# Gating z where the projection's tiles leave PSUM, key rows and index scores in one block, prompt attention with turning three steps behind

## The chip, the cores and the metric

One core of one Trainium2 chip runs the kernel. The metric is device time in microseconds (us) from the start to the end of one execution, and the number compared is the median of several runs. Engine names: TensorE (PE in the rows, its weight loads PEld), VectorE (DVE), ScalarE (ACT), GpSimd (POOL), SyncE (SP, issues DMAs). A "q" behind a name (SPq, ACTq) marks what the engine's sequencer issues.

## The reference

One inference step of a two-layer decoder: a prompt of 512 tokens and 8 sample sequences of one token each (a past of 2048). Layer 0 has two attention mixers on one input projection; layer 1 is a gated convolution. For this change the following matters, in the reference's own lines (cut):

```
def att_project(h, w_in):
...
    proj = h @ w_in
...
    ga = jax.nn.sigmoid(ga).reshape(b, t, G_A, R_A, 3)
...
    wi = wi * (H_IDX ** -0.5)
...
def dsa_select(qi, wi, kidx, t, topk):
    dots = jnp.einsum('bqhd,bld->bqhl', qi, kidx, preferred_element_type=jnp.float32) * (D_IDX ** -0.5)
    score = jnp.einsum('bqh,bqhl->bql', wi.astype(jnp.float32), jax.nn.relu(dots))
...
def att_merge(ga, za, zb, o_cmp, o_slc, o_win, o_b, w_out):
    b, t = za.shape[:2]
    o_a = ga[..., 0:1] * o_cmp + ga[..., 1:2] * o_slc + ga[..., 2:3] * o_win
    o_a = o_a.reshape(b, t, -1) * jax.nn.silu(za)
    o_b = o_b.reshape(b, t, -1) * jax.nn.silu(zb)
    return jnp.concatenate([o_a, o_b], axis=-1) @ w_out
```

The projection's columns are split into qa, kc, vc, ks, vs, kw, vw, ga, za, qb, kb, vb, qi, wi, ki and zb; the new rows of the keys and values and of ki are outputs of their own. silu(z) = z / (1 + exp(-z)). za and zb are 8 heads of 128 columns each, so 16 of the projection's 66 tiles are z tiles.

## The kernel before, in words

Activations lie transposed: 128 rows of features by 520 columns (512 prompt tokens, 8 sample tokens; `TC = 520`). The work is a row of stages; each is one block with a program per engine, and ends with the clearing of its semaphores and a barrier of all engines (`stage`, L90).

**Projection** (`stage_project`, L474). 66 tiles of 128 output columns. For tile t ScalarE makes the high part of the weights (`hi`, L128), VectorE the low part (`lo`, L133), TensorE runs 96 matmuls (L146), ScalarE copies the left half of PSUM to `pj_out` (L567) and VectorE the right half (L609), GpSimd stores the tile to the DRAM tensor `proj` (L635). Weight parts have two buffers, so `hi` and `lo` of tile t+2 start when tile t is done and are needed when tile t+1 is done. After every second tile TensorE also does two slots of the next conditioning product (L199). `SEGS` cuts the 16 rounds of four tiles into loops.

**Rows** (`stage_rows`, L647). Nine groups of key or value tiles, then the tile of gates (`GW`), are loaded from `proj` (L667 to L671), turned by TensorE (L687, L688), copied by VectorE (L704 to L708) and stored to the outputs from ScalarE's queue (L718, L722). SyncE waits for each load to land before it issues the next.

**Sample queries** (`stage_sample_queries`, L726). The sigmoid of the gates, one load of all tiles' sample columns (`sT`, L736, 8320 runs of 32 bytes), ten small loads of gates through DRAM (L740 to L744) issued by SyncE, and 33 small VectorE instructions (L773 to L779).

**Index scores of the prompt** (`stage_index_prompt`, L798). For 16 heads: load q (L817), four matmuls (L831), Relu on ScalarE (L842), multiply-add on VectorE (L854); at the end GpSimd cuts the diagonal (L863). Then the stage of sample index scores begins (L912, `stage_index_sample`).

**Prompt attention** (`stage_attend_prompt`, L1699), once for mixer A (two branches) and once for B. Two groups of four heads; a head is 8 (A) or 4 (B) units of 128 query rows with 128 to 512 keys. A step t in program order: TensorE does the logits of unit t (L1790), turns the probabilities of unit t-DT (L1804) and multiplies those of unit t-DV by the values (L1818). VectorE adds bias and takes the maximum (L1877 in A; L1880 and L1883 in B), negates it (L1885), then normalizes unit t-1 (L1892, L1896 or L1898). ScalarE scales the queries of the next head (L1827), takes exp (L1846) and copies turned probabilities out of PSUM (L1860). In A a compressed branch comes with each head's first unit (L1786, L1815). z of a head: exp on ScalarE (L1830), plus one on GpSimd (L1995), the reciprocal on VectorE in four (A) or two (B) pieces, one a step (L1905), times z on GpSimd (L1997), and the product with the attention output at the head's end (L1948, L1950). `SL` is the number of heads whose loads have a buffer: 2 in A, 4 in B. Loads of a head wait for the head that used the buffer to finish (`fin`).

```
DP, DT, DV, ring = 1, 2, 3, 4
SL = 2 if A else 4
```

Of the kernel before, what the change touches and what calls it, by code (L numbers as in the profile page):

```python
# [473 lines left out]
def stage_project(k):  # L474
# [7 lines left out]
    SEGS = [(0, 1, 0, 0, 2 * D), (1, 4, 512, 0, 2 * D + 512), (4, 5, 2048, 1, 0), (5, 13, 2584, 1, 512), (13, 14, 2584 + 8 * 512, 1, 9 * 512), (14, 16, 7208, 1, 10 * 512)]  # L482
# [12 lines left out]
    with ExitStack() as ctx:  # L495
# [3 lines left out]
        heads = k.sb("pj_heads", [2 * NH, BREV], ctx=ctx)  # L499
        ada = Ada(k, ctx, 4, "1")  # L500
        with nc.Block() as block:
# [57 lines left out]
            def _(act):  # L559
# [8 lines left out]

                def body(j, seg):
                    for s in range(4):  # L570
                        step(4 * seg[0] + s, j, first=(seg[0] == 0))
                    ada.keep_rows(act, ada_entry(4 * seg[0] + 3), seg[0], j, 2)
                    if seg[0] == 5:
                        copies(j)
# [21 lines left out]
                step(64, 0)  # L596
                step(65, 0, last=True)
# [32 lines left out]
            def _(pool):  # L630

                def store(t, j4, tile):
                    pool.wait_ge(kept_a, j4 + (t + 3))
                    pool.wait_ge(kept_v, j4 + (t + 3))
                    pool.dma_start(tile, out[:, t % 4, :]).then_inc(stored[t % 4], 16)  # L635

                with pool.Fori(0, 16) as j:
# [7 lines left out]


def stage_rows(k):  # L647

    nc, ps = k.nc, k.psum
    tile_in, turned, rows_kept, rows_out, table_in = (k.sem(f"rw_{n}") for n in ("tile_in", "turned", "rows_kept", "rows_out", "table_in"))  # L650
    pairs = [(KC, "cmp_k"), (VC, "cmp_v"), (KS, "slc_k"), (VS, "slc_v"), (KW, "win_k"), (VW, "win_v"), (KB, "dsa_k"), (VB, "dsa_v"), (KI, "idx_k")]
    with ExitStack() as ctx:
# [3 lines left out]
        with nc.Block() as block:  # L656

            @block.sync
            def _(sp):
                sp.dma_start(k.pages[:, :], k.i["page_table"].rearrange("(o s) p -> o (s p)", o=1)).then_inc(table_in, 16)  # L660
                sp.dma_start(k.hot[:, :], k.i["hot"][:, T:O_ALL]).then_inc(table_in, 16)
                for n, (tile, name) in enumerate(pairs + [(GW, None)]):
                    if n >= 2:

                        sp.wait_ge(turned, n - 1)
                    if name == "idx_k":
                        sp.dma_start(src[:, n % 2, 0, :], k.proj[tile]).then_inc(tile_in, 16)  # L667
                    elif name:
                        sp.dma_start(src[:, n % 2, :, :], k.proj[tile:tile + 2].rearrange("g p c -> p g c")).then_inc(tile_in, 16)
                    else:  # L670
                        sp.dma_start(src[:, n % 2, 0, :], k.proj[tile]).then_inc(tile_in, 16)  # L671

                    sp.wait_ge(tile_in, 16 * (n + 1))
                sp.wait_ge(table_in, 32)

            @block.tensor
            def _(pe):
                for n, (tile, name) in enumerate(pairs + [(GW, None)]):
                    pe.wait_ge(tile_in, 16 * (n + 1))

                    if n >= 2:
                        pe.wait_ge(rows_kept, 2 * (n - 1))
                    width, parts = P, 2 if name and name != "idx_k" else 1
                    for g in range(parts):
                        for i in range(TT):
                            at = i * 256 + g * P
                            pe.transpose(ps[:, 3 * (n % 2) + at // 512, at % 512:at % 512 + width], src[0:width, n % 2, g, i * P:(i + 1) * P], k.ident[0:width, 0:width])  # L687
                        mm = pe.transpose(ps[0:NS, 3 * (n % 2) + 2, g * P:g * P + width], src[0:width, n % 2, g, T:TC], k.ident[0:width, 0:width])  # L688
                    mm.then_inc(turned, 1)

            @block.vector
            def _(dve):
                for n, (tile, name) in enumerate(pairs + [(GW, None)]):
# [1863 lines left out]
```

## Time and profile before

| what | value |
|---|---|
| three runs | 3378.32, 3385.72, 3390.58 us (median 3385.72) |
| the profiled execution: its own time | 3371.94 us |
| its span in the trace | 3370.3 us |
| busy: PE / PEld / DVE / ACT / POOL | 88 / 78 / 41 / 21 / 3 % of the span |
| mean granted TensorE clock | 0.927 of full speed |
| DMA, mean | 147 GB/s |

How to read it: the profiled execution is one run, 13.8 us below the median of the three. The mean shares cover stages with different limits, so the rows below are by stage. The stages that the change touches lie, in us from the span's start, at about 145 to 985 (projection), 985 to 1028 (rows), 1028 to 1044 (sample queries), 1044 to 1100 (index scores), 1844 to 2043 (mixer A) and 2043 to 2163 (mixer B). A wait is put down to what came last.

### The profile page before, as it was taken

How to read it: one execution, taken by the hardware profiler on the slowest of the kernel's cores; microseconds unless marked ns; L12 is line 12 of the kernel's file. 1: busy time of each engine (PE TensorE's matmuls, PEld its weight loads, DVE VectorE, ACT ScalarE, POOL GpSimd, SP SyncE). 2: the span in 40 equal slices, each digit the busy share in tenths (PEclk: the TensorE clock that was granted, in tenths of full speed). 3: DMA queues.
4: the chain of work that ended last, by engine and by line, in shares of the span. 5: the costliest groups of instructions: out<-in, count | busy, mean ns of one | idle time of the engine just before them, and what ended most of it. 6: DMA issues, size and time to landing. Idle time of an engine off the chain costs nothing. (4 is left out here: it accounts for less than half of the span.)

```text
span 3370.3 us, 56792 instructions
## 1 busy us (share of the span) xinstructions
PE 2977.2 (88%) x22144; PEld 2631.9 (78%) x22144; DVE 1373.4 (41%) x2245; ACT 708.3 (21%) x1084; POOL 108.4 (3%) x150
## 2 busy tenths in 40 slices
PE   6799999999975889897887775599799999999897
PEld 3599999999963478786553554499699999999897
DVE  2322222212214368465741666633533343333433
ACT  2211111211102021120000443321322222222222
POOL 0000000000000000000000112100000000000000
PEclk8799999999987899897986887799899999999998
DMA  9765676777544732333897223343233333334331
GB/s 342 229 188 168 196 219 209 224 220 218 172 130 125 209 117 61 108 100 96 276 303 248 79 95 129 111 131 87 66 95 104 94 93 92 104 93 114 108 89 51
DMA packets 594867, 496.75 MB, mean 147 GB/s; under 512 B 37148, under 2 KB 515885, under 8 KB 593885
## 3 DMA queue, kind: packets, MB, share of 16 engines
q1 hardware_dynamic: 528408, 408.45, 41.3%
q10 hardware_dynamic: 58496, 60.59, 5.5%
q0 software_dynamic: 7840, 26.10, 2.0%
q8 instruction: 75, 1.23, 0.2%
q14 instruction: 48, 0.39, 0.0%
HBM read 460.02 MB, written 48.70 MB: 151 GB/s over the span
## 5 line engine op out<-in xcount | busy, mean ns | idle before, releaser
L146 PE MATMUL psum<-h_high,w_high 128*128 128x260 f32 x4992 | 1009.3, 283 | 21.6 <-DVE w_low L133 21.6
L146 PE MATMUL psum<-h_high,w_low 128*128 128x260 f32 x4992 | 1006.9, 283 | 0.0
L146 PE MATMUL psum<-h_low,w_high 128*128 128x260 f32 x4992 | 1005.2, 283 | 0.0
L146 PEld LDWEIGHTS psum<-h_high,w_high 128*128 128x128 f32 x4992 | 770.5, 189 | 35.9 <-issue 30.1
L146 PEld LDWEIGHTS psum<-h_high,w_low 128*128 128x128 f32 x4992 | 770.7, 189 | 0.0
L146 PEld LDWEIGHTS psum<-h_low,w_high 128*128 128x128 f32 x4992 | 768.9, 189 | 0.0
L133 DVE TENSOR_TENSOR w_low<-w,w_high 128x2048 fp32r<-128x2048 f32 x162 | 370.9, 2291 | 591.6 <-ACT w_high L128 591.6
L128 ACT ACTIVATE w_high<-w 128x2048 fp32r<-128x2048 f32 x162 | 309.2, 1910 | 479.5 <-PE psum L146 361.3
L609 DVE COPY pj_out<-psum 128x260 f32<-128x260 f32 x66 | 28.3, 429 | 429.8 <-PE psum L146 429.8
L567 ACT ACTIVATE pj_out<-psum 128x260 f32<-128x260 f32 x66 | 25.6, 388 | 593.9 <-PE psum L146 593.9
L199 PE MATMUL psum<-w,c 128*32 128x512 f32 x768 | 105.3, 661 | 26.1 <-DMA w<-in_w_ada 17.5
L1041 PE MATMUL psum<-w_v,cz_xtv 128*128 128x256 f32 x512 | 118.9, 394 | 0.0
L1041 PE MATMUL psum<-w,cz_xtk 128*128 128x256 f32 x512 | 117.9, 392 | 0.0
L1041 PEld LDWEIGHTS psum<-w_v,cz_xtv 128*128 128x128 f32 x512 | 116.3, 309 | 1.3
L1041 PEld LDWEIGHTS psum<-w,cz_xtk 128*128 128x128 f32 x512 | 115.7, 309 | 0.7
L1583 DVE COPY at_kt<-psum 128x512 f32<-128x512 f32 x144 | 93.0, 686 | 35.1 <-PE psum L1383 34.2
L2094 DVE TENSOR_TENSOR ou_t<-psum,adaT 128x8 f32<-128x8 f32 x32 | 5.3, 165 | 199.1 <-PE psum L146 187.0
L2376 DVE RECIPROCAL cv_parts<-cv_parts 128x520 f32<-128x520 f32 x16 | 54.5, 3405 | 71.9 <-ACT cv_parts L2310 71.9
L199 PEld LDWEIGHTS psum<-w,c 128*32 128x32 f32 x768 | 20.0, 114 | 71.4 <-issue 40.3
L166 PE MATMUL psum<-h_high,w_high 128*128 128x260 f32 x192 | 41.9, 302 | 34.7 <-DVE h_low L2061 22.9
L1818 PE MATMUL psum<-pa_ptA,pa_vA 128*128 128x128 f32 x320 | 54.7, 308 | 14.4 <-ACT pa_ptA L1860 14.4
L635 POOL DMA_DIRECT2D proj<-pj_out x66 | 35.9, 545 | 939.7 <-DVE pj_out L609 939.7
(374 smaller groups left out, 2829.2 us busy)
## 6 DMA issues: line engine op xcount, KB each, us to landing
w<-in_w_ada SPq DMA_DIRECT2D x96, 1024.0 KB, 8.1
w<-in_w_in_att SPq DMA_DIRECT2D x65, 1024.0 KB, 11.7
w<-in_w_in_conv SPq DMA_DIRECT2D x64, 1024.0 KB, 6.3
proj<-pj_out POOLq DMA_DIRECT2D x66, 260.0 KB, 5.0
cz_pgk<-in_cache_nsa_cmp_k SPq DMA_DIRECT2D x128, 128.0 KB, 2.1
cz_pgv<-in_cache_nsa_cmp_v SPq DMA_DIRECT2D x128, 128.0 KB, 2.2
w<-in_w_out_att SPq DMA_DIRECT2D x16, 1024.0 KB, 6.4
w<-in_w_out_conv SPq DMA_DIRECT2D x16, 1024.0 KB, 6.3
```

Of the source, the lines that this page charges most:

```text
L128: act.activation(k.wh[:, s % 2, :], k.w[:, n % 4, :], ACT.Copy).then_inc(self.high, 1)
L133: dve.tensor_tensor(k.wl[:, s % 2, :], k.w[:, n % 4, :], k.wh[:, s % 2, :].bitcast(F32), ALU.subtract).then_inc(k.w_free[n % 4], 1)
L146: mm = pe.matmul(k.psum[:, banks + hf, 0:HC], w[:, kt, :], x[:, kt, hf * HC:(hf + 1) * HC], start=(kt == 0 and m == 0), stop=(kt == KT - 1 ...
L166: mm = pe.matmul(k.psum[:, banks[i] + hf, 0:HC], w[:, kt, :], x[:, kt, hf * HC:(hf + 1) * HC], start=(kt == 0 and m == 0), stop=(kt == KT ...
L199: mm = pe.matmul(k.psum[32 * a:32 * a + 32, self.bank, :], k.c32[:, q * 4 + a, :], k.w[:, n % 4, a * 512:(a + 1) * 512], start=(q == 0), s ...
L567: nc.scalar.activation(out[:, t % 4, 0:HC], ps[:, t % 2 * 2, 0:HC], ACT.Copy).then_inc(kept_a, 1)
L609: dve.tensor_copy(out[:, t % 4, HC:TC], ps[:, t % 2 * 2 + 1, 0:HC]).then_inc(kept_v, 1)
L635: pool.dma_start(tile, out[:, t % 4, :]).then_inc(stored[t % 4], 16)
L1041: mm = pe.matmul(ps[:, b, 0:CH], rows, w1[:, l, :], start=(l == 0), stop=(l == CB - 1))
L1583: dve.tensor_copy(kt[:, s % 2, :, c * 256:(c + 1) * 256], ps[:, 3 + q % 2, :].rearrange("p (g q) -> p g q", g=G)).then_inc(kept, 1)
L1818: mm = pe.matmul(ps[:, o, i * P:(i + 1) * P], hv[:, r % SL, br, c, :], pt[:, v % ring, c * P:(c + 1) * P], start=(not A and v % UH == 0 an ...
L2376: dve.reciprocal(e[:, :], e[:, :]).then_inc(zrecip, 1)
```

## The change

It has three parts. (1) z / (1 + exp(-z)) is computed in the projection: for each of the 16 z tiles ScalarE takes exp of the tile after both copies, GpSimd adds one, VectorE takes the reciprocal, GpSimd multiplies, and then the tile is stored; `SEGS` has two more cuts, so that z tiles fall into rounds of their own, and GpSimd's loop follows the same rounds. (2) The stages of rows, sample queries and index scores become one block: the gates' tile comes first, two tile loads may be in flight, the sample columns are loaded after the second tile, ScalarE's queue issues the ten gate loads, and the small VectorE instructions for the sample queries come after the index loop. (3) Prompt attention loads z already gated: exp, plus one, reciprocal and product with z go; `SL` is 4 in both mixers; `DT, DV` become 3 and 5.

```diff
-    SEGS = [(0, 1, 0, 0, 2 * D), (1, 4, 512, 0, 2 * D + 512), (4, 5, 2048, 1, 0), (5, 13, 2584, 1, 512), (13, 14, 2584 + 8 * 512, 1, 9 * 512), (14, 16, 7208, 1, 10 * 512)]
+    SEGS = [(0, 1, 0, 0, 2 * D), (1, 4, 512, 0, 2 * D + 512), (4, 5, 2048, 1, 0), (5, 7, 2584, 1, 512), (7, 13, 2584 + 2 * 512, 1, 3 * 512), (13, 14, 2584 + 8 * 512, 1, 9 * 512),
+            (14, 15, 7208, 1, 10 * 512), (15, 16, 7208 + 512, 1, 11 * 512)]
...
+    zexp, zone, zrec, zdone = (k.sem("pj_" + n) for n in ("zexp", "zone", "zrec", "zdone"))
+    def gate(r0, s):
+        tile = 4 * r0 + s
+        return tile - ZA if ZA <= tile < ZA + 8 else tile - ZB + 8 if ZB <= tile < ZB + 8 else None
...
+        ez = k.sb("pj_ez", [P, 2, TC], ctx=ctx)
...
+                def exp_gate(t, j):
+                    n = gate(t // 4, t % 4)
+                    if n is not None:
+                        act.wait_ge(kept_a, j * 4 + (t + 3))
+                        act.wait_ge(kept_v, j * 4 + (t + 3))
+                        act.wait_ge(zdone, j * 4 + (n + 1))
+                        nc.scalar.activation(ez[:, t % 2, :], out[:, t % 4, :], ACT.Exp, scale=-1.0).then_inc(zexp, 1)
...
-                    if seg[0] == 5:
-                        copies(j)
+                    if seg[0] in (5, 7):
+                        copies(j + (seg[0] - 5))
...
+                exp_gate(64, 0)
...
+                    n = gate(t // 4, t % 4)
+                    if n is not None:
+                        dve.wait_ge(zone, j * 4 + (n + 1))
+                        dve.reciprocal(ez[:, t % 2, :], ez[:, t % 2, :]).then_inc(zrec, 1)
...
+                def store(t, j):
+                    n = gate(t // 4, t % 4)
+                    if n is None:
+                        pool.wait_ge(kept_a, j * 4 + (t + 3))
+                        pool.wait_ge(kept_v, j * 4 + (t + 3))
+                    else:
+                        z = ez[:, t % 2, :]
+                        pool.wait_ge(zexp, j * 4 + (n + 1))
+                        settle(k, pool)
+                        pool.tensor_scalar(z, z, 1.0, None, ALU.add).then_inc(zone, 1)
+                        pool.wait_ge(zrec, j * 4 + (n + 1))
+                        pool.tensor_tensor(out[:, t % 4, :], out[:, t % 4, :], z, ALU.mult).then_inc(zdone, 1)
+                        pool.wait_ge(zdone, j * 4 + (n + 3))
+                    to = k.proj[t] if t >= 64 else k.proj[bass.ds(j * 4 + t, 1)].rearrange("o p c -> (o p) c")
+                    pool.dma_start(to, out[:, t % 4, :]).then_inc(stored[t % 4], 16)
...
+def stage_rows_and_index(k):
...
+    tiles = [(GW, None)] + pairs
...
+                for n, (tile, name) in enumerate(tiles):
+                    if n >= 2:
+                        sp.wait_ge(turned, n - 1)
+                    if parts(name) == 2:
+                        sp.dma_start(src[:, n % 2, :, :], k.proj[tile:tile + 2].rearrange("g p c -> p g c")).then_inc(tile_in[n % 2], 16)
+                    else:
+                        sp.dma_start(src[:, n % 2, 0, :], k.proj[tile]).then_inc(tile_in[n % 2], 16)
+                    if n == 1:
+                        sp.dma_start(k.pages[:, :], k.i["page_table"].rearrange("(o s) p -> o (s p)", o=1)).then_inc(table_in, 16)
+                        sp.dma_start(k.hot[:, :], k.i["hot"][:, T:O_ALL]).then_inc(table_in, 16)
+                        sp.dma_start(k.sT[:, :, :], k.proj[0:GW, :, T:TC].rearrange("t p s -> p t s")).then_inc(got, 16)
                 sp.dma_start(ki[:, :], k.proj[KI]).then_inc(k_in, 16)
+                sp.wait_ge(gated, 2)
+                sp.dma_start(k.gate_rows, k.gws[:, :]).then_inc(out, 16)
...
+                sp.wait_ge(table_in, 32)
...
+                    if n >= 2:
+                        pe.wait_ge(kept, 2 * (n - 1))
...
+                pe.wait_ge(kept, 2 * len(tiles))
...
+                act.wait_ge(kept, 2)
+                nc.scalar.activation(k.gw[:, :, 0:NGA], k.gw[:, :, 0:NGA], ACT.Exp, scale=-1.0).then_inc(k.s_sig, 1)
+                nc.scalar.activation(k.gws[:, 0:NGA], k.gws[:, 0:NGA], ACT.Exp, scale=-1.0).then_inc(k.s_sig, 1)
...
+                    act.dma_start(k.o[name + "_p"].rearrange(flat, p=P), rows[:, n % 2, :, 0:width]).then_inc(rows_out[n % 2], 16)
...
+                act.wait_ge(out, 16)
+                act.dma_start(k.ga_s[:, :], k.gate_rows[:, 0:NGA].rearrange("s (h b) -> s h b", b=3)).then_inc(back, 16)
+                act.dma_start(k.wi_s[:, :], k.gate_rows[:, NGA:NGW].unsqueeze(2)).then_inc(back, 16)
+                for c in range(4):
+                    for sh in range(2):
+                        act.dma_start(k.ga_4[32 * c:32 * c + 32, sh, :], k.gate_rows[4 * sh:4 * sh + 4, 0:NGA].rearrange("s (h b) -> s h b", b=3)).then_inc(back, 16)
...
+                    if n >= 3:
+                        dve.wait_ge(rows_out[n % 2], 32 * ((n - 1) // 2))
...
+                    if n == 2:
+                        dve.wait_ge(k.s_sig, 2)
...
+                        dve.tensor_scalar(k.gws[:, NGA:NGW], k.gws[:, NGA:NGW], NI ** -0.5, None, ALU.mult).then_inc(gated, 1)
+                dve.wait_ge(gated, 2)
...
+                dve.wait_ge(got, 16)
+                dve.wait_ge(zero, 2)
...
+                        dve.tensor_scalar(own, k.sT[:, tile:tile + NH, s].rearrange("p (g h) -> p g h", g=G), SCALE, None, ALU.mult).then_inc(step, 1)
...
+                    dve.tensor_scalar(k.qpi[:, h:h + 144 * 7 + 1:144], k.sT[:, QI + h, :], SCALE, None, ALU.mult).then_inc(step, 1)
+                dve.wait_ge(back, 160)
+                dve.tensor_scalar(k.wsel[:, :], k.const[:, C_BD16:C_BD16 + NS], k.wi_s[:, 0:1], None, ALU.mult).then_inc(step, 1)
+                dve.wait_ge(step, 1 + 2 * NH + NI)
...
-    SL = 2 if A else 4
-    names = ("in0", "in1", "in2", "in3", "scaled", "qk", "added", "neg", "exp", "recip", "prob", "turned", "kept", "pv", "head", "fin", "ez", "zstep",
...
-    DP, DT, DV, ring = 1, 2, 3, 4
-    ZP = 4 if A else 2
...
+    DP, DT, DV, ring = 1, 3, 5, 4
...
-                def exp_z(r):
-                    nc.scalar.activation(e[:, r % SL, :], hz[:, r % SL, :], ACT.Exp, scale=-1.0).then_inc(ez, 1)
...
-                def recip_z(g, r, q):
-                    if q == 0:
-                        dve.wait_ge(zstep, g * (2 * HG) + (2 * r + 1))
-                    part = e[:, r % SL, q * (TC // ZP):(q + 1) * (TC // ZP)]
-                    dve.reciprocal(part, part).then_inc(zrecip, 1)
...
-                    dve.wait_ge(zstep, g * (2 * HG) + (2 * r + 2))
...
-                    dve.tensor_tensor(y[:, 0:T], ps[:, 4 + r % 2, :], e[:, r % SL, 0:T], ALU.mult)
+                    dve.tensor_tensor(y[:, 0:T], ps[:, 4 + r % 2, :], hz[:, r % SL, 0:T], ALU.mult)
...
-                        pool.wait_ge(ez, g * HG + (r + 1))
-                        settle(k, pool)
-                        pool.tensor_scalar(z, z, 1.0, None, ALU.add).then_inc(zstep, 1)
-                        pool.wait_ge(zrecip, g * (ZP * HG) + ZP * (r + 1))
-                        pool.tensor_tensor(z, hz[:, r % SL, :], z, ALU.mult).then_inc(zstep, 1)
...
-            with k.stage():
-                stage_rows(k)
...
-                            stage_sample_queries(k)
-                        with k.stage():
-                            stage_index_prompt(k)
+                            stage_rows_and_index(k)
                         with k.stage():
```

## Rows read from the trace of the kernel before

**Rows 1.** Windows: busy us (count) of PE, PEld, DVE, ACT, POOL; clock, DMA share, GB/s

```profile
400.00:500.00 100.00, 100.00 (x833) 93.71 (x832) 21.97 (x18) 19.17 (x18) 4.34 (x8) 1.00 0.66 202
...
985.00:1024.50 39.50, 21.81 (x90) 16.16 (x90) 13.55 (x21) 0.00 (x0) 0.00 (x0) 0.50 0.77 236
...
1000.00:1010.00 10.00, 5.70 (x25) 4.03 (x24) 4.63 (x6) 0.00 (x0) 0.00 (x0) 0.50 0.90 288
...
1028.00:1044.00 16.00, 0.00 (x0) 0.00 (x0) 4.01 (x39) 1.68 (x3) 2.16 (x4) 0.50 0.33 18
```

**Rows 2.** Timeline of VectorE in the projection: start us, us, engine, line, instruction

```profile
400.83 0.43 DVE L609 COPY pj_out<-psum 128x260 f32<-128x260 f32 x1 [7.04 <-PE psum L146]
403.03 2.29 DVE L133 TENSOR_TENSOR w_low<-w,w_high 128x2048 fp32r<-128x2048 f32 x1 [1.77 <-ACT w_high L128]
412.26 0.43 DVE L609 COPY pj_out<-psum 128x260 f32<-128x260 f32 x1 [6.94 <-PE psum L146]
```

**Rows 3.** One tile, gated z of mixer A: count, duration ns min/median/max, first and last start

```profile
L1905 DVE RECIPROCAL pa_eA<-pa_eA x32: 956/959/961, 1864.0 to 2029.1; 128x130 f32<-128x130 f32 x32
L1830 ACT ACTIVATE pa_eA<-pa_zA x8: 619/624/627, 1855.9 to 2012.1; 128x520 f32<-128x520 f32 x8
L1995 POOL TENSOR_SCALAR pa_eA<-pa_eA x8: 1504/1506/1528, 1856.8 to 2012.9; 128x520 f32<-128x520 f32 x8
L1997 POOL TENSOR_TENSOR pa_eA<-pa_zA,pa_eA x8: 1280/1287/1293, 1873.5 to 2030.2; 128x520 f32<-128x520 f32 x8
```

**Rows 4.** Timeline, rows to index scores; last, a DMA issue (count, KB, us to landing)

```profile
985.32 0.26 SPq L660 DMA_DIRECT2D pages<-in_page_table  x1
...
1024.57 0.15 DVE L705 COPY gws<-psum 8x16 f32<-8x16 f32 x1
...
1036.30 1.26 DVE L775 TENSOR_SCALAR qpi<-sT 128x8 f32<-128x8 f32 x16
...
1048.85 7.00 PE L831 MATMUL psum<-ip_k,ip_q 128*128 128x128 f32 x16 [24.70 <-DMA ip_q<-proj]
...
1095.26 1.94 DVE L854 SCALAR_TENSOR_TENSOR mask<-ip_relu,gw,mask 128x128 f32<-128x128 f32 x4 [0.63 <-ACT ip_relu L842]
...
rw_src<-proj SPq DMA_DIRECT2D x8, 520.0 KB, 3.8
```

**Rows 5.** Tiles of mixer A, first and last start, and ScalarE's wait: total us, times, longest

```profile
L1786 PE MATMUL psum<-kcmp,pa_qA x64: 182/374/388, 1856.1 to 2014.4; 128*128 x64
...
L1950 DVE TENSOR_TENSOR pa_yoA<-oS,pa_eA x8: 153/156/157, 1887.2 to 2037.8; 128x8 f32<-128x8 f32 x8
...
ACT pa_qA L1827 <- DMA pa_vcA<-vcmp_rows: 86.5, 5, 68.2
```

**Rows 6.** Timeline of VectorE in mixer A: first instruction of three consecutive steps

```profile
1889.40 0.49 DVE L1877 CUSTOM_DVE_ANT_0 pa_sA<-psum,pa_tA 128x384 f32<-128x384 f32 x1
...
1891.59 0.63 DVE L1877 CUSTOM_DVE_ANT_0 pa_sA<-psum,pa_tA 128x512 f32<-128x512 f32 x1
...
1893.17 0.68 DVE L1877 CUSTOM_DVE_ANT_0 pa_sA<-psum,pa_tA 128x512 f32<-128x512 f32 x1
```

**Rows 7.** Windows in mixer A (first row) and mixer B (second), columns as in Rows 1

```profile
1876.00:1894.00 18.00, 14.47 (x88) 9.80 (x86) 15.26 (x58) 7.17 (x23) 3.34 (x3) 1.00 0.30 94
...
2062.00:2074.00 12.00, 8.78 (x38) 6.54 (x38) 9.69 (x25) 4.61 (x15) 1.70 (x2) 0.77 0.00 0
```

**Rows 8.** Mixer B: tiles (first and last start), then groups by form (busy us, mean ns)

```profile
L1790 PE MATMUL psum<-pa_kB,pa_qB x64: 275/592/847, 2050.6 to 2147.8; 128*128 128x128 f32 x16, 128*128 128x256 f32 x16, 128*128 128x384 f32 x16, 128*128 128x512 f32 x16
...
L1950 DVE TENSOR_TENSOR pa_yoB<-oS,pa_eB x8: 156/157/158, 2074.6 to 2158.4; 128x8 f32<-128x8 f32 x8
...
L1905 DVE RECIPROCAL pa_eB<-pa_eB 128x260 f32<-128x260 f32 x16 | 28.4, 1772 | 0.0
...
L1883 DVE CUSTOM_DVE_ANT_0 pa_sB<-pa_sB,mask 128x512 f32<-128x512 f32 x8 | 9.4, 1175 | 1.5 <-DVE pa_sB L1880 1.5
...
L1883 DVE CUSTOM_DVE_ANT_0 pa_sB<-pa_sB,mask 128x384 f32<-128x384 f32 x8 | 4.5, 559 | 1.5 <-DVE pa_sB L1880 1.5
```

More of the change, by code:

```diff
@@ L630, in _, with body @@
             def _(pool):
[L632 to L637, printed above, removed]
+                def store(t, j):
[13 more added lines that the diff above has]
+                    pool.dma_start(to, out[:, t % 4, :]).then_inc(stored[t % 4], 16)
+                def body(j, seg):
                     for s in range(4):
-                        store(s, j * 4, k.proj[bass.ds(j * 4 + s, 1)].rearrange("o p c -> (o p) c"))
+                        store(4 * seg[0] + s, j)
+                pool.sem_inc(zdone, 2)
+                rounds(pool, body)
                 for t in range(64, NTILES):
-                    store(t, 0, k.proj[t])
+                    store(t, 0)
                 for s in range(4):
@@ L644, in stage_project, with settle, off @@
     k.ring = project_entry(NTILES - 1) + 1
-def stage_rows(k):
+def settle(k, eng):
+    eng.sem_inc(k.settled[eng.engine], 1)
+def off(i):
+    return P * (i * (i + 1) // 2)
+def stage_rows_and_index(k):
     nc, ps = k.nc, k.psum
-    tile_in, turned, rows_kept, rows_out, table_in = (k.sem(f"rw_{n}") for n in ("tile_in", "turned", "rows_kept", "rows_out", "table_in"))
     pairs = [(KC, "cmp_k"), (VC, "cmp_v"), (KS, "slc_k"), (VS, "slc_v"), (KW, "win_k"), (VW, "win_v"), (KB, "dsa_k"), (VB, "dsa_v"), (KI, "idx_k")]
+    tiles = [(GW, None)] + pairs
+    table_in, turned, kept = (k.sem(f"rw_{n}") for n in ("table_in", "turned", "kept"))
+    tile_in, rows_out = ([k.sem(f"rw_{n}{b}") for b in range(2)] for n in ("tile_in", "out"))
+    got, zero, gated, step, out, back = (k.sem(f"sq_{n}") for n in ("got", "zero", "gated", "step", "out", "back"))
+    q_in, mm_done, relu_done, added, cut = [k.sem("ip_q_in0"), k.sem("ip_q_in1")], *(k.sem(f"ip_{n}") for n in ("mm", "relu", "added", "cut"))
+    k_in = k.sem("ip_k_in")
     with ExitStack() as ctx:
@@ L788, in settle @@
-def settle(k, eng):
-    eng.sem_inc(k.settled[eng.engine], 1)
-def off(i):
-    return P * (i * (i + 1) // 2)
-def stage_index_prompt(k):
-    nc, ps = k.nc, k.psum
-    q_in, mm_done, relu_done, added, step = [k.sem("ip_q_in0"), k.sem("ip_q_in1")], *(k.sem(f"ip_{n}") for n in ("mm", "relu", "added", "step"))
-    k_in = k.sem("ip_k_in")
-    with ExitStack() as ctx:
         q = k.sb("ip_q", [P, 2, TC], ctx=ctx)
@@ L807, in stage_index_prompt, with parts @@
         sc = k.mask
+        def parts(name):
+            return 2 if name and name != "idx_k" else 1
         with nc.Block() as block:
@@ L823, in _ @@
                 pe.sem_inc(relu_done, 2)
+                for n, (tile, name) in enumerate(tiles):
+                    pe.wait_ge(tile_in[n % 2], 16 * (n // 2 + 1))
+                    if n >= 2:
+                        pe.wait_ge(kept, 2 * (n - 1))
+                    for g in range(parts(name)):
+                        for i in range(TT):
+                            at = i * 256 + g * P
+                            pe.transpose(ps[:, 3 * (n % 2) + at // 512, at % 512:at % 512 + P], src[:, n % 2, g, i * P:(i + 1) * P], k.ident)
+                        mm = pe.transpose(ps[0:NS, 3 * (n % 2) + 2, g * P:(g + 1) * P], src[:, n % 2, g, T:TC], k.ident)
+                    mm.then_inc(turned, 1)
+                pe.wait_ge(kept, 2 * len(tiles))
                 pe.wait_ge(k_in, 16)
@@ L843, in _ @@
                         ins.then_inc(relu_done, 1)
+                for b in range(2):
+                    act.wait_ge(rows_out[b], 32 * len([n for n in range(1, len(tiles)) if n % 2 == b]))
             @block.vector
```

172 lines of the change are left out of this document (48 added, 124 removed).

## The prediction

> **What bounds the kernel now.** I read the windows by stage first, then the timelines of the stages that the change touches, then waits and groups of the prompt attention. In the projection TensorE is busy 100.00 of 100 us at full clock (1.00, 2.4 GHz), VectorE 22 and ScalarE 19 [rows 1]: work added there beside TensorE is free as long as the next weights are ready in time. In the rows stage TensorE is busy 21.8 of 39.5 us at half clock (0.50, 1.2 GHz) while the DMA engines are at 0.77, and at 0.90 in its middle [rows 1]: loads and stores are the limit. Between the last row copy (1024.57) and the first index matmul (1048.85) TensorE does nothing for 24.3 us [rows 4]; that is the sample queries and two stage ends. In mixer A a full-clock window has TensorE at 14.47 of 18 us and VectorE at 15.26 [rows 7]: neither is full, they wait for each other, and four times ScalarE stands for a load (86.5 us in 5 waits, the first of 68.2 lies ahead of the stage, so 18.3 inside it [rows 5]). In mixer B VectorE leads with 9.69 of 12, and TensorE's mean clock is 0.77 [rows 7].
>
> **Part 1, gating in the projection: 0 us.** Sixteen times, counted from a tile's end: both copies 0.43 [rows 2], exp 0.62, plus one on GpSimd 1.51, reciprocal 4 x 0.959 less what four short instructions cost over one, taken in full as 3.84, then `lo` of tile t+2, which now stands behind that reciprocal in VectorE's order, 2.29 [rows 2, 3]. That is 8.7; with four hand-overs at 0.2 (L1883 stood 1.5 us in 8 for its own engine's last result [rows 8]), 9.5. GpSimd's product (1.29) runs beside `lo`; if `lo` has to wait for all of it, 10.8. TensorE needs `lo` of t+2 one tile later, and two tile ends lie 412.26 - 400.83 = 11.4 us apart, more where conditioning slots lie between [rows 2]. The cover is thin (0.6 to 1.9 us) but there. Without it the cost would be the excess, 16 times. `hi` of t+2 stands behind the exp, 1.2 us later, and is still ahead of `lo`. The freeing of the weight buffer, and so SyncE's next weight load, comes up to 6 us later, in a stage that asks for a new megabyte only when a whole tile has passed. GpSimd's store of a z tile leaves some 8 us later; `pj_out` has four buffers, so 34 us of cover. Two more loops and GpSimd's rounds: 0, since TensorE's loops show no gap [rows 1].
>
> **Part 2, rows and index in one block: 23 us off.** The transfers set the pace. They keep the DMA engines 0.77 x 39.5 = 30.4 us, and the window with the `sT` load 0.33 x 16 = 5.3 [rows 1]; 35.7 at the best share seen, 0.90, is 39.7 us. The last two tiles' stores (3.7 by the same share) need not land first, and the last tile is turned and copied in 2.5. So the index matmuls start at 985.3 + 39.7 - 3.7 + 2.5 = 1023.8 in place of 1048.85 [rows 4]: 25 us earlier; k, q and the gates' way through DRAM pass underneath. At share 1.0 it is 1020; if `sT` blocks the rows for its own length, 1029. The Trainium skill ("DMA: Bandwidth & Descriptors", section "Issuing engines are not separate DMA queues") says that transfers from all queues interleave on the same sixteen engines, so that more queues save issue time only. By that rule the two loads in flight gain next to nothing and the stage saves the 23 us below; by landing times alone (3.8 us a load [rows 4], five pairs, and the 2.5) the index would start at 1006.8 and part 2 would save 40.
>
> New waits: TensorE waits for all twenty row copies before the first index matmul, with nothing else queued. SyncE waits for the gates ahead of the q loads, and those are done at the third tile. ScalarE waits for the gates in DRAM and then issues ten loads ahead of the first Relu: about 5 us against the 3.5 us of the first head's matmuls (7.00 for two heads [rows 4]) and two stores; I take 0.7. VectorE's 32 small instructions follow the index loop: the 16 for qpi took 1.26 us [rows 4], so 2.5, with wsel 2.9, of which GpSimd's cuts covered 1.2 before: 1.7 more. 25.1 - 0.7 - 1.7 = 22.7. The index loop itself (1048.85 to 1097.2) is unchanged.
>
> **Part 3a, mixer A: 30 us off.** The stage runs from 1856.1 to 2037.9, 181.8 us [rows 5]. Four heads of buffers take away the 18.3 us of load waits; SyncE's loads go out up to two heads earlier, beside transfers that need 0.3 of the engines [rows 7]. Each head loses 4 x 0.959 on VectorE [rows 3]: a step with a piece of it took 1891.59 - 1889.40 = 2.19 us with 384 keys, a step without it 1.58 with 512 [rows 6]. Of the 18.6 us of a head without a load wait, VectorE then needs 15.26 - 3.84 = 11.4 and its gaps, about 13; TensorE needs 14.47 x 18.6 / 18 = 15.0 and its gaps, so TensorE becomes the bound. Turning three steps behind gives its instructions a whole step more before they need VectorE, so I take 16.5 a head. What is left of the stage, 181.8 - 18.3 - 8 x 18.6 = 14.7, is two fillings and drains; two more steps in the drain add 2.5 a group. 8 x 16.5 + 14.7 + 5 = 151.7: 30 off. Bounds: the load waits alone, 18; a head at 15.4, 39.
>
> **Part 3b, mixer B: 30 us off.** 2050.6 to 2158.4 is 107.8 us, 13.5 a head [rows 8]. A head loses 2 x 1.772, and the reduction over 512 keys, which ran beside GpSimd's passes at 1175 ns, goes to 559 x 512 / 384 = 745 [rows 8]: 3.97 together, 31.8 for eight; I take 30, as the drain grows. Lower bound: TensorE keeps its clock of 0.77 and then needs 8.78 of 12 us, 9.5 a head with no gap and some 11.1 with them: 19 off. Upper: VectorE's work without gaps, and the lockstep gone, 8.7 a head: 38. `SL` is unchanged in B; GpSimd's stores, no longer behind its two passes, leave earlier, which nobody waits for.
>
> **Sum.** 0 + 23 + 30 + 30 = 83 off. The profiled execution took 3371.94 us, which would be 3289; it lies 13.8 below the median of the runs shown, so on the median 3385.72 - 83 = 3303. A difference of 0.3% (10 us) is about what a measurement of this kernel can tell from none.
>
> **Rivals.**
> (a) *The prompt stages stay in lockstep*: TensorE at its present clock becomes the bound and only the load waits and the lower bound in B are won: 18 + 19 + 23 = 60 off, 3326. For it: B's clock of 0.77 with 8.78 of 12 us busy [rows 7]; against it: in A, with 14.47 of 18 busy, the clock is 1.00 [rows 7]. Chance 0.20.
> (b) *The sample columns hold up the rows*: 5 us of DMA time for 260 KB, in 8320 runs, now lies amid the row loads; index starts at 1029 and part 2 gives 17, with A a little short: 70 off, 3316. For it: 18 GB/s at a share of 0.33 [rows 1]. Chance 0.15. The Trainium skill (same page, section "Why small descriptors are slow (HBM only)") gives a fixed cost per packet as the reason; the row agrees.
> (c) *Both prompt stages reach their upper bounds*: 39 + 38 + 26 = 103 off, 3283. For it: VectorE is the only engine near full in B. Chance 0.18.
> (d) *The gate chain holds up the projection*, the side of slower: place, `lo` behind the reciprocal; price, the excess over 11.4 us, sixteen times. To undo 83 us the chain must last 11.4 + 83 / 16 = 16.6 us, against 9.5 to 10.8; were each of its four passes to take twice its time, it would be 17.4 and the kernel 3399. Against it: the same four instructions are measured, in a stage where GpSimd and VectorE also meet [rows 3]. Chance 0.04, half of it too small to undo the whole gain.
> (e) *The change does not do what it says*: the deeper turning frees nothing, because VectorE's reciprocal was the only cause of the waits; then only A is a little short, 77 off, which is inside my forecast's own range and its chance.
>
> **How the numbers follow.** The forecast, 3303 with its own range of 3293 to 3313, has 0.43; (a), (b), (c), (d) as given. To hold eight in ten the range reaches from (c) to (a) and takes in the bounds: 17 + 18 + 19 = 54 off, 3332, and 103 off, 3283; rounded outward by 2 to 3 us for the scatter of the runs, 3280 to 3334. Only (d) is not faster, and is split between the two other outcomes: faster by over 0.3% 0.96, within 0.3% 0.02, slower 0.02.
>
> **What would show it.** Projection: TensorE still 100 of 100 us busy, and `lo` after a z tile ending 9 to 11 us behind the tile's end; a gap on TensorE at each z tile would be (d). Rows: DMA share at 0.9 over the stage, first index matmul near 1024, the stage after it 23 us earlier; near 1029 is (b). Mixer A: no wait of L1827 for a load, head period 16 to 17, TensorE over 0.9 busy at clock 1.00. Mixer B: about 78 us, VectorE full. I am wrong if the two prompt stages together give less than 37 us or more than 77.

## The result, and the profile after

| what | before | after |
|---|---|---|
| median of four runs each, us | 3382.02 (3374.29 to 3390.58) | 3270.40 (3262.51 to 3271.61) |
| ratio of after to before | | 0.9669, 95% interval 0.9654 to 0.9685 |
| the profiled execution: own time, span, us | 3371.94, 3370.3 | 3262.51, 3260.9 |

The kernel became faster by some 112 us; 83 were forecast, and the time lies below the low end of the forecast's range (3280 to 3334). By the two traces the span fell by 109.4 us: the block of rows and index scores gave 18.8 (mixer A's first matmul at 1837.3 in place of 1856.1), mixer A 52.3 (129.5 us long in place of 181.8), mixer B 37.8 (70.1 in place of 107.9). All the rest together gave 0.5. The forecast had 23, 30 and 30 for the three.

Windows of the kernel after, columns as in [rows 1]: one gap between z tiles in the projection; the block in two halves; two middle heads of mixer A; all of A; all of B.

```profile
401.00:412.40 11.40, 11.40 (x99) 10.91 (x101) 5.98 (x3) 2.83 (x3) 5.35 (x3) 1.00 0.20 54
984.00:1006.00 22.00, 9.56 (x45) 7.43 (x45) 7.44 (x17) 0.39 (x2) 2.08 (x4) 0.58 0.95 192
1006.00:1027.00 21.00, 9.97 (x45) 7.55 (x45) 8.59 (x12) 0.00 (x0) 0.00 (x0) 0.58 0.90 294
1851.80:1880.50 28.70, 28.29 (x182) 20.60 (x181) 23.24 (x111) 18.03 (x55) 1.10 (x2) 1.00 0.26 81
1837.00:1966.00 129.00, 119.82 (x720) 86.09 (x720) 93.07 (x438) 72.53 (x216) 3.81 (x7) 0.95 0.35 112
1979.00:2049.00 70.00, 55.08 (x304) 38.70 (x304) 54.12 (x207) 35.53 (x104) 3.78 (x7) 0.91 0.46 151
```

The projection is as full as in [rows 1]. The block keeps the DMA engines at 0.90 to 0.95 from end to end. Two middle heads of A fill the window of 28.7 us, 14.35 each, with TensorE busy in 28.29 of it; in [rows 7] it was 14.47 of 18.

The kernel before, mixer A in steps of 18 us (the first four) and the whole stage:

```profile
1856.00:1874.00 18.00, 15.38 (x51) 9.26 (x51) 11.61 (x48) 6.21 (x20) 2.03 (x2) 0.62 0.17 53
1874.00:1892.00 18.00, 14.61 (x91) 10.38 (x90) 15.15 (x58) 9.00 (x27) 2.53 (x3) 1.00 0.19 57
1892.00:1910.00 18.00, 13.30 (x68) 10.33 (x67) 9.36 (x45) 7.39 (x22) 3.08 (x3) 0.81 0.19 64
1910.00:1928.00 18.00, 12.58 (x58) 9.33 (x57) 10.34 (x38) 6.63 (x19) 3.33 (x3) 0.81 0.36 117
...
1856.00:2038.00 182.00, 142.12 (x720) 100.32 (x720) 121.89 (x472) 76.25 (x223) 26.16 (x23) 0.86 0.24 77
```

The window of [rows 7] was one of the good ones (1.00, the 2.4 GHz level throughout). Over the stage the clock was 0.86, and the same 720 matmuls kept TensorE busy 142.1 us there and 119.8 after, at 0.95. So busy time is no fixed amount of work. Part of this difference is the clock; what is left of it at one clock stands in the section on the prediction.

Timeline of VectorE and GpSimd in the projection after, first of the two z tiles that [rows 2] show without gating:

```profile
400.44 0.43 DVE L628 COPY pj_out<-psum 128x260 f32<-128x260 f32 x1 [5.62 <-PE psum L146]
403.50 3.40 DVE L632 RECIPROCAL pj_ez<-pj_ez 128x520 f32<-128x520 f32 x1 [2.63 <-POOL pj_ez L664]
406.82 2.23 DVE L133 TENSOR_TENSOR w_low<-w,w_high 128x2048 fp32r<-128x2048 f32 x1
411.87 0.43 DVE L628 COPY pj_out<-psum 128x260 f32<-128x260 f32 x1 [2.82 <-PE psum L146]
...
406.99 3.23 POOL L666 TENSOR_TENSOR pj_out<-pj_out,pj_ez 128x520 f32<-128x520 f32 x1 [3.52 <-DVE pj_ez L632]
...
969.98 1.30 POOL L666 TENSOR_TENSOR pj_out<-pj_out,pj_ez 128x520 f32<-128x520 f32 x1 [3.52 <-DVE pj_ez L632]
```

`lo` ends at 409.05, 8.6 us after the tile (forecast 9.5), and VectorE then idles 2.8 us.

The block of rows and index scores after: SyncE's issues, then one copy of VectorE and TensorE's first index matmuls.

```profile
986.44 0.43 SPq L733 DMA_DIRECT2D sT<-proj  x1
988.91 4.27 SPq L727 DMA_DIRECT2D rw_src<-proj  x1
...
997.80 1.12 PE L757 MATMUL psum<-const,rw_src 128*128 128x128 f32 x4 [5.76 <-DMA rw_src<-proj]
...
1025.88 0.69 DVE L819 COPY rw_rows<-psum 128x512 f32<-128x512 f32 x1 [4.32 <-DMA out_dsa_k_s<-rw_rows_s]
...
1027.07 1.78 PEld L767 LDWEIGHTS psum<-ip_k,ip_q 128*128 128x128 f32 x6 [5.94 <-issue]
```

The tile load behind `sT` takes 4.27 us to issue (0.34 to 0.43 is usual), TensorE waits 5.76 us for its tile, and the last copy waits 4.32 us for a store before it. The index matmuls start at 1027.1; forecast 1023.8, before 1048.85 [rows 4].

### The profile page after: what moved, and what is told of

It is laid out like the page before. It is cut to its first block and busy times, and to the rows that moved or that the text cites. A ratio compares the mean times of both kernels' runs of the same rounds, so it can differ in the third digit from the quotient of the medians.

```text
span 3260.9 us, 56498 instructions
## 1 busy us (share of the span) xinstructions
PE 2934.2 (90%) x22144; PEld 2601.3 (80%) x22144; DVE 1365.2 (42%) x2213; ACT 710.9 (22%) x1085; POOL 131.6 (4%) x150
## 5 line engine op out<-in xcount | busy, mean ns | idle before, releaser
L628 DVE COPY pj_out<-psum 128x260 f32<-128x260 f32 x66 | 28.3, 429 | 380.3 <-PE psum L146 380.3
L166 PE MATMUL psum<-h_high,w_high 128*128 128x260 f32 x192 | 41.9, 301 | 34.2 <-DVE h_low L2036 22.4
L632 DVE RECIPROCAL pj_ez<-pj_ez 128x520 f32<-128x520 f32 x16 | 54.5, 3403 | 40.3 <-POOL pj_ez L664 40.3
```

The lines of the kernel that those rows point to most:

```text
L166: mm = pe.matmul(k.psum[:, banks[i] + hf, 0:HC], w[:, kt, :], x[:, kt, hf * HC:(hf + 1) * HC], start=(kt == 0 and m == 0), stop=(kt == KT ...
L632: dve.reciprocal(ez[:, t % 2, :], ez[:, t % 2, :]).then_inc(zrec, 1)
```

## Experiments

Each kernel was measured beside the kernel before on the same chip; "ratio" is to that, with its 95% interval, and after stands at 0.9669. Mixer A's length is counted from its first matmul to the end of the last product with z, as in [rows 5]; a head's time is from its first matmul to the first one of the next head.

### Undoing the depth alone

```diff
-    DP, DT, DV, ring = 1, 3, 5, 4
+    DP, DT, DV, ring = 1, 2, 3, 4
```

> The kernel after with DT, DV back at 2 and 3 in both mixers; all else as after. Theory (the clock): mixer A is bound by TensorE at 14.4 us a head once VectorE's reciprocals and the load waits are gone, and its clock no longer falls in stalls; depth only removes short waits. Then A's head period stays under 15.2 us, A is at most 6 us longer, B at most 6, and the kernel is 0 to 12 us slower than after. Rival (depth): the two steps of slack are what closes the gaps; A's head goes to 16.5 us or more and B's up by 1 us, and the kernel is 24 to 33 us slower than after.

Ratio 0.9751 (0.9734 to 0.9767), so 28 us slower than after. A takes 150.4 us with middle heads of 17.0, B 77.3. The rival holds: with z out and four heads of buffers, depth is worth 21 us in A and 7 in B. Two middle heads of A, then the longest wait of each of TensorE's two queues in A for another engine's result inside the stage (total us, times, longest):

```profile
1864.75:1898.82 34.07, 29.62 (x183) 20.90 (x181) 23.82 (x111) 18.21 (x55) 1.10 (x2) 1.00 0.36 117
```
```profile
PEld psum L1803 <- DVE pa_sA L1889: 31.9, 40, 1.7
PE psum L1803 <- DVE pa_sA L1889: 13.8, 21, 1.5
```

At the same clock (1.00) as after and with the same work on VectorE (23.8 us here, 23.2 after), TensorE is busy 29.6 of 34.1 us. It waits at the turning for probabilities that VectorE is still making: 40 and 21 times, up to 1.7 us. In the kernel after the same waits are 12.2 and 0.6 us in the whole of A.

### Two heads of buffers in A

```diff
-    SL = 4
+    SL = 2 if A else 4
```

> The kernel after with two heads of buffers in mixer A in place of four; turning still three steps behind. Theory (the clock): the load waits come back, longer than before since a head now ends two steps later (about 8 us each in place of 4.6, four to six times), and TensorE's clock falls behind each of them as in the kernel before (0.62 to 0.81 in half of its 18 us windows): A 45 to 65 us longer than after, mean clock in A under 0.88. Rival (waits cost their own length): A longer by the load waits alone, 18 to 30 us, with the clock in A as in after, 0.95.

Ratio 0.9786 (0.9766 to 0.9807), 40 us slower than after; A takes 168.2.

```profile
ACT pa_qA L1826 <- DMA pa_vcA<-vcmp_rows: 107.2, 6, 67.8
```
```profile
1840.00:2008.00 168.00, 131.97 (x719) 99.83 (x719) 95.08 (x440) 72.10 (x215) 3.80 (x7) 0.84 0.27 83
```

The first row is ScalarE's wait for loads, as in [rows 5]: the longest one lies ahead of the stage, the other five are 39.4 us, against 18.3 in the kernel before. A is 38.7 us longer than after, which has no such wait inside the stage. So the waits cost their own length, and the fall of the clock (to 0.84, from 0.95 after) adds nothing visible to it. Of the theory the growth of the waits and the fall of the clock held, but not the surcharge for that fall. The rival was right in kind, and wrong in size and in the clock.

### The eight combinations in mixer A

Three more kernels complete the table of what is in place: z out of the stage, four heads of buffers, depth. Four heads of buffers alone:

```diff
-    SL = 2 if A else 4
+    SL = 4
...
-        hvc = k.sb("pa_vc" + tag, [NCB // 4, 2, P], ctx=ctx)
+        hvc = k.sb("pa_vc" + tag, [NCB // 4, SL, P], ctx=ctx)
```

> The kernel before with four heads of buffers in mixer A and nothing else. Theory (the clock): without the 18.3 us of load waits the clock in A rises from 0.86 to 0.93 or more, and A gains more than the waits, 25 to 40 us. Rival (waits cost their own length): 15 to 20 us. Second rival (the reciprocal on VectorE keeps the lockstep): under 10 us, the load waits being replaced by waits for VectorE.

z out alone (after with `SL = 2 if A else 4` and DT, DV = 2, 3):

> The kernel after with two heads of buffers in A and DT, DV at 2 and 3: of the prompt stages only z is gone. Theory (the clock): the load waits stay, so do the falls of the clock; A gains 10 to 20 us on the kernel before of the 52 that after gains, B 28 to 36, and the kernel is 55 to 75 us faster than before. Rival (VectorE's reciprocal is the main cause in A): A gains 30 us or more, the kernel is 80 us or more faster than before.

Depth alone in A (`DP, DT, DV, ring = (1, 3, 5, 4) if A else (1, 2, 3, 4)` in the kernel before):

> The kernel before with DT, DV = 3, 5 in mixer A alone (mixer B stays at 2, 3); z and two heads of buffers stay. Theory (the three parts work only together: slack is of use when neither a load nor the reciprocal holds a whole head up): the load waits grow, since a head ends two steps later and its buffers come free later, and eat what the depth gives; mixer A between 6 us shorter and 10 us longer than the 181.8 of before. Rival (the parts add): depth gives its 21 us, as between e1 and after, and A takes 161.

Depth and four heads of buffers, z left in the stage (both edits in the kernel before):

> The kernel before with four heads of buffers and DT, DV = 3, 5 in mixer A; z stays in the prompt stages. Theory (TensorE becomes the bound as soon as it has slack, whether or not VectorE still does the reciprocal: 11.4 + 3.8 us of VectorE a head are just over TensorE's 14.4): a head of 15.2 to 16.2, mixer A 136 to 145 us, 36 to 46 us faster than before; moving z is then worth only 7 to 15 us of A. Rival (the reciprocal sets A's pace): A stays above 152, under 30 us faster than before.

| kernel | z out | buffers | depth | A, us | middle head, us | ratio |
|---|---|---|---|---|---|---|
| before | | | | 181.8 | 20 to 24 | 1 |
| depth alone | | | x | 194.6 | 27 to 28 | 1.0034 (1.0020 to 1.0048) |
| buffers alone | | x | | 159.4 | 18.3 | 0.9926 (0.9904 to 0.9947) |
| buffers and depth | | x | x | 156.2 | 16.4, 17.6 | 0.9928 (0.9908 to 0.9948) |
| z alone | x | | | 178.7 | 22 to 25 | 0.9835 (0.9810 to 0.9859) |
| z and depth | x | | x | 168.2 | 21 to 25 | 0.9786 (0.9766 to 0.9807) |
| z and buffers | x | x | | 150.4 | 17.0 | 0.9751 (0.9734 to 0.9767) |
| after | x | x | x | 129.5 | 14.4 | 0.9669 (0.9654 to 0.9685) |

The ratios of the four kernels with z out hold the block, the projection and mixer B too. In A z alone is worth 3.1 us, buffers alone 22.4, depth alone costs 12.8; together they are worth 52.3. z and buffers together are worth 31.4. With four heads of buffers, depth gives 3.2 us while z is in the stage (159.4 to 156.2) and 20.9 when it is out (150.4 to 129.5). With two heads of buffers and z in, depth is a loss: a head ends two steps later and its buffers come free later. ScalarE's waits for loads in that kernel, the longest ahead of the stage:

```profile
ACT pa_qA L1827 <- DMA pa_vcA<-vcmp_rows: 116.1, 6, 67.5
```

Inside the stage these are 48.6 us, against 18.3 in the kernel before.

Against what was expected: buffers alone lay between theory (25 to 40) and rival (15 to 20). z alone missed in A (3 in place of 10 to 20; the load waits inside the stage grew from 18.3 to 23.9 us) and fitted in B (79.6 us, 28 less). Depth alone did more harm than expected (12.8, at most 10 expected). With buffers and depth the theory, 136 to 145 us, fell and the rival, above 152, held. The reason shows in that last kernel: two windows of its mixer A, and VectorE's three longest waits there.

```profile
1874.00:1893.00 19.00, 16.49 (x103) 11.55 (x101) 16.84 (x65) 10.22 (x30) 4.53 (x4) 1.00 0.03 4
1893.00:1912.00 19.00, 15.87 (x98) 11.16 (x99) 16.61 (x65) 10.86 (x33) 3.88 (x4) 1.00 0.43 130
```
```profile
DVE pa_sA L1877 <- PE psum L1790: 16.3, 1, 16.3
DVE pa_yoA L1948 <- PE psum L1818: 11.1, 2, 5.7
DVE pa_sA L1896 <- DVE pa_stA L1892: 10.0, 64, 0.2
```

The wait of 16.3 is the start of the stage, the two of 11.1 us together are the ends of the two groups, and 10.0 is VectorE's wait for its own last result, 64 times. In between it waits for no other engine: with z in the stage, VectorE (busy 16.8 and 16.6 of 19 us) sets the pace once buffers and depth hold nothing up. With z out it needs 11.6 us a head (half of the 23.24 after), and TensorE, with 14.15, takes over.

### The block undone

The three stages of before (rows, sample queries, index scores) in the kernel after.

> The kernel after with rows, sample queries and index scores as the three stages of before. Theory: the block is worth its 18 us wherever the rest stands: 17 to 20 us slower than after, the first index matmul some 64 us behind the last projection store as in before. Rival (part of the gain belongs to the shorter stage behind it or is given back): under 13 us.

Ratio 0.9732 (0.9712 to 0.9752), 21 us slower than after, and A starts at 1855.6, 18.3 us later, within the 17 to 20 of the theory. The block is worth what the traces said.

### The sample columns moved, and taken away

```diff
-                        sp.dma_start(k.sT[:, :, :], k.proj[0:GW, :, T:TC].rearrange("t p s -> p t s")).then_inc(got, 16)
                 sp.dma_start(ki[:, :], k.proj[KI]).then_inc(k_in, 16)
+                sp.dma_start(k.sT[:, :, :], k.proj[0:GW, :, T:TC].rearrange("t p s -> p t s")).then_inc(got, 16)
```

> The kernel after with the load of the sample columns (8320 runs of 32 bytes) issued behind the last tile load and the index keys in place of behind the second tile. Theory (the columns hold up the rows): the tile loads no longer stand behind it, the first index matmul starts 3 to 6 us earlier than 1027.1 and the kernel is 3 to 6 us faster than after, unless the first q load, now behind the columns on the same queue, takes the gain back. Rival (DMA work is the limit, whatever its order): within 1.5 us of after.

SyncE's issues in this kernel:

```profile
984.03 0.34 SPq L729 DMA_DIRECT2D rw_src<-proj  x1
...
988.01 20.15 SPq L727 DMA_DIRECT2D rw_src<-proj  x7
1011.64 0.35 SPq L729 DMA_DIRECT2D rw_src<-proj  x1
1012.03 0.43 SPq L733 DMA_DIRECT2D ip_k<-proj  x1
1012.51 0.43 SPq L734 DMA_DIRECT2D sT<-proj  x1
1012.98 6.92 SPq L737 DMA_DIRECT2D gate_rows<-gws  x1
```

The last tile load is issued 27.6 us behind the first (32.9 after), and now the issue behind `sT`, that of the gates, takes 6.92 us. The first index matmul comes 39.3 us behind the first load (42.2 after), and mixer A starts 3.7 us earlier from there. The columns do hold up the rows. In the time nothing of that is to be seen, ratio 0.9675 (0.9656 to 0.9695): the intervals are wider than the effect.

In the next kernel GpSimd copies the eight columns of each ungated tile into place during the projection, and the load goes:

```diff
+                        if t < 64:
+                            settle(k, pool)
+                            pool.tensor_copy(k.sT[:, bass.ds(j * 4 + t, 1), :].rearrange("p o s -> p (o s)"), out[:, t % 4, T:TC]).then_inc(columns, 1)
...
-                        sp.dma_start(k.sT[:, :, :], k.proj[0:GW, :, T:TC].rearrange("t p s -> p t s")).then_inc(got, 16)
```

> The kernel after without the load of the sample columns: GpSimd copies the eight columns of each tile that is not gated into place in the projection, 49 copies of 128x8. Theory (DMA work is the limit in the block of rows and index scores, 35.7 engine-us of which 5.3 are the columns): the first index matmul 5 to 7 us earlier than the 42.2 us behind the first load in after, the kernel 4 to 7 us faster than after; more than the 2.9 us that moving the load gave. Rival (the waits of VectorE for the stores before it are the limit): under 3.5 us, as in the kernel with the load moved.

The first index matmul comes 37.1 us behind the first load, 5.1 earlier than after, within the 5 to 7 of the theory. In the time it stays unproved: ratio 0.9670 (0.9654 to 0.9686). In the profiled execution the first load comes 2.2 us later than after; scatter is enough for that, since the kernel with only the depth undone has the projection of after and its first load comes 2.4 us later too.

### The gating chain made longer

```diff
+                        dve.reciprocal(spare[:, t % 2, :], ez[:, t % 2, :])
                         dve.reciprocal(ez[:, t % 2, :], ez[:, t % 2, :]).then_inc(zrec, 1)
```

> The kernel after with one more reciprocal of 3.4 us on VectorE in the gating of each of the 16 z tiles, its result unused. Theory (the chain has 2.8 us of cover at a short tile, 1.4 where a weight load came late): the chain becomes 3.4 us longer, half of the sixteen tile ends are short, so the excess of 0.6 to 2 us is paid 8 times: 4 to 14 us slower than after, with gaps on TensorE behind z tiles. Rival (there is slack that the rows do not show, or the excess is made up in the longer tiles): within 3 us of after, TensorE without gaps.

Ratio 0.9669 (0.9653 to 0.9685), the same as after: the rival holds. VectorE, behind the same tile as above:

```profile
400.63 0.43 DVE L629 COPY pj_out<-psum 128x260 f32<-128x260 f32 x1 [5.62 <-PE psum L146]
403.69 3.40 DVE L633 RECIPROCAL pj_spare<-pj_ez 128x520 f32<-128x520 f32 x1 [2.63 <-POOL pj_ez L666]
407.01 3.34 DVE L634 RECIPROCAL pj_ez<-pj_ez 128x520 f32<-128x520 f32 x1
410.27 2.23 DVE L133 TENSOR_TENSOR w_low<-w,w_high 128x2048 fp32r<-128x2048 f32 x1
412.42 0.41 DVE L629 COPY pj_out<-psum 128x260 f32<-128x260 f32 x1
```

TensorE's timeline at the next tile's end:

```profile
411.63 0.40 PE L146 MATMUL psum<-h_high,w_low 128*128 128x260 f32 x2
411.95 1.92 PE L199 MATMUL psum<-w,c 128*32 128x512 f32 x16
413.81 1.06 PE L213 MATMUL psum<-const,ada_rows 128*128 128x9 f32 x8
414.72 0.48 PE L146 MATMUL psum<-h_high,w_high 128*128 128x260 f32 x2
```

`lo` now ends at 412.50, 11.9 us after its tile and past the next tile's end, and VectorE no longer idles ahead of its copy. TensorE has matmuls of the conditioning product to do first: the weights are needed at 414.72 and not at 411.95. In the whole projection it waited for `w_low` once, 0.2 us, and was busy 824.0 of 825 us between 150 and 975 (824.3 after).

### A version that is faster still

One pass of eight heads in place of a loop over two groups of four, so that the pipeline isn't drained between them (cut):

```diff
-    HG = NH // G
+    HG = NH
+    KV = NH // G
...
-                with pe.Fori(0, G) as g:
+                for g in (0,):
...
-                            load(hk[:, b, br, :], k.proj[bass.ds(g + kt, 1), :, 0:T].rearrange("o p c -> (o p) c"))
+                            load(hk[:, b, br, :], k.proj[bass.ds(r // KV + kt, 1), :, 0:T].rearrange("o p c -> (o p) c"))
```

> The kernel after with the eight heads of a prompt stage written out as one pass in place of a loop over two groups of four: no draining and filling between the fourth and the fifth head. Theory (what is left over TensorE's head period of 14.4 us is fill and drain): the step from head four to head five, 20.4 us in mixer A, goes to 14.4, and the head after it from 15.65 to 14.4; mixer A 6 to 8 us shorter, B 4 to 6, the kernel 9 to 14 us faster than after. Rival (a written-out program pays for its instructions, or the loads of head five wait for buffers): under 4 us, or slower.

Ratio 0.9629 (0.9613 to 0.9645), 13.5 us faster than after. A takes 118.7, B 67.8: more than expected in A, less in B. The step from the fourth head to the fifth, 20.4 us after, is 14.1, and the middle heads became shorter too, 13.9 in place of 14.4.

With that, the columns kept in the projection, and three buffers for the loaded tiles and the turned rows:

> One pass of eight heads, sample columns kept in the projection, and three buffers in place of two for the loaded tiles and the turned rows. Theory: the two gains add, 9 to 14 and 4 to 7, and the third buffer gives 1 to 3 more since DMA work is then near its limit: 14 to 24 us faster than after. Rival: the third buffer only moves the wait to the DMA engines, and the sum is 13 to 18.

3242.02 us, ratio 0.9599 (0.9583 to 0.9615), 23.7 us faster than after. The first index matmul comes 30.2 us behind the first load (42.2 after), the stage behind the block 9.7 us earlier; A takes 118.9, B 67.4. That is the top of the expected range: less the columns' 5.1 and 5.2 us, the third buffer gave 6.9 at the first index matmul and 4.5 at the stage behind, where 1 to 3 were expected. With two buffers and the columns kept VectorE waited 14.6 us for turned tiles and 3.2 for stores; with three it is 2.6 and 8.4: the loads ran further ahead.

## Why the prediction was right and wrong

**Part 3a, mixer A, is the step that failed: "I take 16.5 a head" and the 19.7 us of fill and drain around it, the two terms in which the deeper turning stood.** Measured are 14.4 a head and 129.5 - 8 x 14.4 = 14.3 around them. Of the 22 us missed, 16.8 are the heads and 5.4 the rest. The depth was priced too low: rival (e), by which it frees nothing, lay only 6 us from the forecast, and undoing it costs 20.9 in A. With z out and four heads of buffers but without depth, A is 31.4 us faster than before, with heads of 17.0 and 150.4 - 8 x 17.0 = 14.4 around them. That this is so near the 30 forecast is chance, since the forecast counted the depth in.

Inside the head two sizes were wrong. The gaps of TensorE were taken as 1.5 us; without depth they are 2.2 (17.0 less 29.62 / 2), with it 0.2. And TensorE's floor of 15.0 was the busy time of a window in which it waits, scaled up; two heads after show 28.29, 14.15 each. At the same clock of 1.00, 88 matmuls took 14.47 us in [rows 7], 0.164 each, and 182 took 28.29 after, 0.155 each. Single matmuls did not become shorter (128x512 logits 594 ns in both windows, 128x128 products with the values 281 and 277), so they overlap more when nothing holds them up. The Trainium skill (Perfetto Trace Analysis, "Identifying the Most-Contended Engine" and the page's opening note) says that matmul busy time is a poor measure of how near a kernel is to its limit because matmuls are pipelined; the trace agrees, with these 0.164 and 0.155 us. The extra 5 us for a longer drain did not show: the rest is 14.4 without depth and 14.3 with it. VectorE's share was right: 11.4 forecast, 11.6 measured.

**The terms do not add.** The prediction priced load waits (18.3) and reciprocals one after the other. In A buffers alone give 22.4 and z alone 3.1, the two together 31.4, and with depth 52.3: what one part gives depends on whether another still holds up a step.

**Part 3b** lacks the same term. 30 was the work taken off VectorE, and z out without depth gives 28.3 and 30.6 in the two kernels that have this mixer B (79.6 and 77.3 us long). Depth gives the rest of the 37.8, 7 to 9.5; kernels with the mixer B of before scatter by 3.4 us (107.9 to 111.4). The whole is at the upper bound, 38. TensorE's clock, 0.77 in [rows 7] and 0.75 over mixer B before, is 0.91 after, so the lower bound's assumption fell. The 9.5 and 8.7 us a head of the two bounds are not worked out there: 8.78 of 12 us would be 9.9 of the 13.5 us of a head. Measured are 8.8 a head, with TensorE busy in 6.9 of them (55.08 / 8).

**Part 2** gave 18.8 in place of 23. The tail was right (54.1 us from the first index matmul to VectorE's first copy in the next stage, 51.3 before; 2.4 forecast and 2.8 measured). The start was 3.3 us late, between the forecast and rival (b)'s 1029: the columns held up the tile loads, and moving them gives 2.9 back. From the first load to the first index matmul the share of the DMA engines is 0.94, better than the 0.90 assumed, but there was more work: 0.94 x 42.2 = 39.7 us in place of 35.7. With the columns' load gone it is 0.87 x 37.2 = 32.4, so they took some 7 us and not 5.3. The share is no hard limit here: between 988.9 and 993, just behind the issue of the columns, the profile counts 1.53. And that the transfers alone set the pace is not shown: with the columns gone, a third buffer saved another 6.9 us.

**Part 1** cost nothing, as forecast, for a better reason than the one given: the chain is 8.6 us, and 3.4 more did no harm. The cover of 11.4 us left out that the conditioning matmuls stand behind the shorter tiles; in the kernel with two reciprocals that puts the need 2.2 us behind the end of `lo`. So rival (d), priced from 11.4, was priced too high. GpSimd's product waits for `lo` and not the other way round, so the 10.8 did not come up.

**Rivals.** (a) fell: B's clock rose, and A's heads went from 20 to 24 us down to 14.4. (e) fell: without depth the kernel is 28 us slower. (c), 103 off, was the nearest, at a chance of 0.18; its bounds came from the same floor of 15.0 and were too low for A by 13 us. The statement that more than 77 us in the two prompt stages would make the prediction wrong came true with 90.

## What to carry to other kernels

TensorE's floor, read from its busy time in a window where it waits, was too high here (15.0 against 14.15): take it from a stretch where the engine runs without gaps, and at the same clock. Removing work, adding buffers and adding slack to a pipeline of several engines are to be priced together, because each shows its worth only when the others no longer hold up a step; here slack cost 12.8 us where buffers were short. Slack that was worth 3 us before VectorE was relieved was worth 21 afterwards.

## What the runs showed of the hardware

GpSimd's product of two 128x520 tiles takes 1.30 us alone (at 969.98, where no `lo` follows) and 3.23 beside `lo`, which started 0.17 us earlier and was not slowed (2.23). The reverse stands in the kernel with depth, buffers and z in the stage: an 8-column product of VectorE takes 0.93 us in place of 0.16 when it starts behind GpSimd's product.

```profile
1925.20 1.28 POOL L1997 TENSOR_TENSOR pa_eA<-pa_zA,pa_eA 128x520 f32<-128x520 f32 x1 [11.62 <-DVE pa_eA L1905]
1925.58 0.93 DVE L1950 TENSOR_TENSOR pa_yoA<-oS,pa_eA 128x8 f32<-128x8 f32 x1
...
1936.56 0.16 DVE L1950 TENSOR_TENSOR pa_yoA<-oS,pa_eA 128x8 f32<-128x8 f32 x1
```

The Trainium skill (SBUF — State Buffer, "SBUF: two separate sides") says that a VectorE instruction with two SBUF inputs and a GpSimd instruction lock a shared pair of ports for their whole length, and the later one waits. Both agree: 409.05 - 406.99 + 1.30 = 3.36 against 3.23, and 1926.48 - 1925.58 + 0.16 = 1.06 against 0.93.

The DMA issue that follows a load of 8320 runs of 32 bytes on SyncE's queue takes 4.27 us (6.92 when moved) in place of 0.34 to 0.43, so this load delays what stands behind it in its queue.

Written out, a head of A takes 13.9 us against 14.4 in a loop over groups, both at clock 1.00; the reason was not tested.
